# A two-layer encoder trunk: x turned raw, its modulation as columns, and the modulation products moved among the pointwise product's tiles

## The reference, cut to what matters

```python
c_act = silu(c)
mod = (c_act @ w_ada[l] + b_ada[l])              # 1024 x 6144 for each layer
sh1, sc1, g1, sh2, sc2, g2 = split(mod, 6)
h = x * (1 + sc1) + sh1
# layer 0: convolution block
u = h @ w_pw1 + b_pw1;  u = u[:, :D] * sigmoid(u[:, D:])     # "pointwise product"
y = depthwise_conv(u, w_dw, 31 taps, causal) + b_dw
y = silu(layer_norm(y)) @ w_pw2 + b_pw2
# layer 1: keys, values (with a modulation of their own, w_ada_kv), queries, attention, w_o
x = layer_norm(ALPHA * x + (1 + g1) * y)
h = x * (1 + sc2) + sh2
y = top2_of_16_experts(h)                        # three 1024 x 1024 matrices for each expert
x = layer_norm(ALPHA * x + (1 + g2) * y)
```

## Time and profile before

| what | value |
|---|---|
| median of 3 runs | 1354.38 us (1353.4 to 1354.49) |
| profiled execution, time | 1353.68 us |
| profiled execution, span of its rows | 1352.0 us |
| PE busy | 1132.6 us (84%) |
| DVE busy | 341.9 us (25%) |
| read from memory | 493.23 MB, 366 GB/s over the span |
| chain that ended last | PE 56%, DMA 37%, DVE 3% |

### The profile page before, as it was taken

The page is one execution under the profiler, slowest core; times in us unless marked ns, Lnnn a source line. Parts: engine busy times, 40 slices in busy tenths (PEclk is TensorE's granted clock), DMA queues, the critical chain, the costliest instruction groups (busy, mean ns, idle before and its releaser), DMA issues.

```text
span 1352.0 us, 16340 instructions
## 1 busy us (share of the span) xinstructions
PE 1132.6 (84%) x6426; PEld 486.6 (36%) x6426; DVE 341.9 (25%) x765; ACT 181.7 (13%) x325; POOL 23.1 (2%) x68
## 2 busy tenths in 40 slices
PE   2699998968998579677879999987899988886686
PEld 0486445322332123222265754532233322321222
DVE  0289433211212111111150152521211121111113
ACT  0001402101111000001010042210101011100001
POOL 3100100000000000000000000000000000000000
PEclk9699998988999889988989999789999999998798
DMA  9905989999999999999995344779999999999993
GB/s 372 409 8 210 419 342 429 424 426 428 427 425 425 427 427 426 426 427 426 421 418 208 125 187 156 304 309 426 427 427 426 395 419 423 429 427 424 429 426 159
DMA packets 43965, 495.70 MB, mean 367 GB/s; under 512 B 4554, under 2 KB 4570, under 8 KB 9570
## 3 DMA queue, kind: packets, MB, share of 16 engines
q1 hardware_dynamic: 42576, 490.75, 86.7%
q10 hardware_dynamic: 690, 2.34, 0.5%
q0 software_dynamic: 608, 1.21, 0.3%
HBM read 493.23 MB, written 1.05 MB: 366 GB/s over the span
## 4 chain that ended last, share of the span: by engine, by line
PE 56%; DMA 37%; DVE 3%; issue 2%; ACTq 1%; SPq 0%; POOL 0%; ACT 0%; POOLq 0%; DVEq 0%
DMA ring<-in_w_up_dram 23%; PE PS L1045 8%; DMA work<-in_w_up_dram 7%; PE PS L863 6%; PE PS L1001 6%; PE PS L1027 5%; PE PS L1142 4%; PE PS L881 4%; PE PS L1069 3%; PE PS L959 3%; PE PS L766 3%; DMA lnrows<-in_ln_ffn_b_dram 3%; DMA work<-in_w_down_dram 2%; PE PS L986 2%; DMA ring<-in_w_down_dram 2%
## 5 line engine op out<-in xcount | busy, mean ns | idle before, releaser
L1045 PE MATMUL PS<-ring,work 128*32 128x512 f32 x1184 | 169.2, 697 | 76.6 <-DMA ring<-in_w_up_dram 52.0
L1001 PE MATMUL PS<-ring,work 128*64 128x512 f32 x640 | 153.4, 624 | 28.6 <-DMA ring<-in_w_gate_dram 19.9
L1045 PEld LDWEIGHTS PS<-ring,work 128*32 128x32 f32 x1184 | 45.3, 125 | 194.8 <-issue 191.2
L1576 DVE TENSOR_TENSOR work<-work,PS 64x512 f32<-64x512 f32 x23 | 15.9, 692 | 320.4 <-ACT work L625 320.4
L1001 PEld LDWEIGHTS PS<-ring,work 128*64 128x64 f32 x640 | 47.0, 143 | 133.0 <-issue 117.1
L863 PE MATMUL PS<-ring,work 128*128 128x512 f32 x192 | 83.1, 593 | 0.0
L1045 PE MATMUL PS<-work 128*32 128x512 f32 x216 | 43.6, 702 | 38.3 <-DMA work<-in_w_up_dram 31.8
L986 PE MATMUL PS<-work 64*128 64x512 f32 x296 | 73.5, 615 | 1.6 <-DVE work L1553 1.6
L625 ACT ACTIVATE work<-PS 64x512 f32<-64x512 f32 x23 | 13.6, 590 | 435.9 <-PE PS L1045 435.9
L959 PE MATMUL PS<-hs,colv 128*64 128x512 f32 x296 | 72.0, 608 | 0.0
L766 PE MATMUL PS<-ring,crep 128*32 128x512 f32 x448 | 58.6, 670 | 15.1 <-DVE crep L1607 12.2
(11 more groups left out here) (276 smaller groups left out, 981.1 us busy)
## 6 DMA issues: line engine op xcount, KB each, us to landing
ring<-in_w_gate_dram SPq DMA_DIRECT2D x52, 2048.0 KB, 37.0
ring<-in_w_up_dram SPq DMA_DIRECT2D x52, 2048.0 KB, 40.5
ring<-in_w_down_dram SPq DMA_DIRECT2D x52, 2048.0 KB, 30.2
ring<-in_w_ada_dram SPq DMA_DIRECT2D x24, 2048.0 KB, 16.9
work<-in_w_gate_dram SPq DMA_DIRECT2D x12, 2048.0 KB, 27.2
ring<-in_w_pw_dram SPq DMA_DIRECT2D x6, 2048.0 KB, 39.6
xs<-in_w_up_dram SPq DMA_DIRECT2D x12, 1024.0 KB, 28.3
work<-in_w_up_dram SPq DMA_DIRECT2D x12, 1024.0 KB, 31.2
```

The lines of the kernel that those rows point to most:

```text
L1001: last = pe.matmul(PS[LARGE * half:LARGE * (half + 1), bank, :], XT[:, kk, LARGE * h:LARGE * (h + 1)], columns(tile, kk, half), start=(h = ...
L1045: last = pe.matmul(PS[SMALL * strip:SMALL * (strip + 1), GATE_BANK, :], XT[:, kk, LARGE * h:LARGE * h + SMALL], columns(load + 2 * h + str ...
```

## The change

1. **x is turned raw.** x is loaded into `hs` instead of `xs`. PE's first work is 16 transposes of it into banks 4 to 7, reading every fourth column. DVE copies x into `xs` in chunk order. After the first modulation third, the shift and scale go through `turn_mod` (4 products) into columns, and ACT and DVE write `hT = x^T * scale + shift` from the transposes. `spread_mod`, `modulate`, `turn_h` and `copy_hT` of this place are gone.
2. **The pointwise product goes tile by tile, with modulation products between.** The first three tiles take each chunk of `w_pw1` as it lands (order j, then f); the tap columns' work lies between these chunks. Then come the second modulation third's first load, tile 3, and the seven others of the second and last third in pairs behind tiles 3 to 6. The last third uses slots 0 to 3 again; so does the modulation of keys and values.
3. **The convolution's first tap** of tiles 0 to 4 moves from DVE to ACT (`begin_conv`); `DVE_STEPS` is a new table, with both `add_ada` in it.
4. **Keys' and values' modulation ahead of `w_pw2`**, in the order of loads and in PE's program: three of its loads lie before the last two products of the mean, one behind them. The mean takes six tiles before it. The bias of `w_pw2` is put first in its accumulation, beside the mean. `turn_ln` lies behind the variance.
5. The residual reads `xs` in contiguous rows; `add_ada` for keys and values is no longer inside the row norm.

```diff
-    L_PW2 = L_ADA0_G2 + ADA_G
-    L_ADAKV = L_PW2 + 2
-    L_ADA1_G0 = L_ADAKV + ADA_G
+    L_ADAKV = L_ADA0_G2 + ADA_G
+    L_PW2 = L_ADAKV + ADA_G
+    L_ADA1_G0 = L_PW2 + 2
...
+        if i in (L_ADA0_G2, L_ADA0_G2 + ADA_G):
+            waiting.rotate(ADA_G)
...
+    others = [i for i in range(LOADS) if layer_of(i) is None]
+    passed_on = others[:L_PW1] + others[L_ADA0_G1:L_ADA0_G2 + ADA_G] + others[L_PW1:L_ADA0_G1] + others[L_ADA0_G2 + ADA_G:]
...
-                act.dma_start(xs[:, t, :], x[0, t * P:(t + 1) * P, :]).then_inc(x_in, 16)
+                act.dma_start(hs[:, t, :], x[0, t * P:(t + 1) * P, :]).then_inc(x_in, 16)
...
-            copy_hT()
+            act.wait_ge(in_cols_copied, 1)
+            for b in (0, 2):
+                act.wait_ge(x_turned, b + 1)
+                for k in (2 * b, 2 * b + 1):
+                    last = act.activation(hT[:, k, :], PS[:, 4 + b, (k % 2) * SEQ:(k % 2 + 1) * SEQ], ACT.Identity,
+                                          scale=cols[:, SCALE, k:k + 1], bias=cols[:, SHIFT, k:k + 1])
+                last.then_inc(hT_even, 1)
+
+            def begin_conv(f):
+                act.wait_ge(u_ready, f + 1)
+                act.activation(CV[:, f, :], U[:, f, 0:SEQ], ACT.Identity, scale=colv[:, f, 0:1],
+                               bias=colv[:, f, ROW_BDW:ROW_BDW + 1]).then_inc(tap_begun, 1)
...
+            pe.wait_ge(x_in, 16 * TT)
+            for b in range(4):
+                for k in (2 * b, 2 * b + 1):
+                    h, kk = divmod(k, KH)
+                    for t in range(TT):
+                        last = pe.transpose(PS[:, 4 + b, (k % 2) * SEQ + t * P:(k % 2) * SEQ + (t + 1) * P],
+                                            hs[:, t, h * HALF + kk:(h + 1) * HALF:KH], ident[:, :])
+                last.then_inc(x_turned, 1)
             pe.wait_ge(c_spread, 1)
...
+            ada(L_ADA0_G0, 0)
             pe.wait_ge(ada_added, 1)
-            spread_mod(modv[0], 1, 4)
-            spread_mod(modv[0], 0, 6)
-            turn_ln(0, 2)
+            turn_mod(modv[0], (0,), TURNED_MODS, 1).then_inc(in_cols_turned, 1)
...
+            for j in range(4):
+                arrived(L_PW1 + j)
+                pe.wait_ge((hT_even, hT_odd)[j % 2], j // 2 + 1)
+                for f in range(3):
+                    gated(f, j)
+                if j == 0:
+                    turn_colrows()
+                if j == 1:
+                    spread_taps()
+            pe.wait_ge(u_ready, 2)
+            ada_load(L_ADA0_G1, 0, 1)
             pe.wait_ge(taps_copied, 3)
...
+            for f in range(3, KD):
+                for j in range(4):
+                    gated(f, j)
+                if f == 3:
+                    ada_load(L_ADA0_G1, 1, 1)
+                    ada_load(L_ADA0_G1, 2, 1)
+                if f == 4:
+                    ada_load(L_ADA0_G1, 3, 1)
+                    ada_load(L_ADA0_G2, 0, 0)
+                if f == 5:
+                    ada_load(L_ADA0_G2, 1, 0)
+                    ada_load(L_ADA0_G2, 2, 0)
+                if f == 6:
+                    ada_load(L_ADA0_G2, 3, 0)
...
-            ada(L_ADA0_G2, 6)
-            pe.wait_ge(ada_added, 2)
-            pe.wait_ge(later_in, LATER)
+            turn_ln(0, 7)
...
-            pe.wait_ge(ada_added, 3)
-            columns_and_turn(0, L_ADAKV)
+            project(L_PW2, 0, y_ready, z_ready, begun=True)
+            columns_and_turn(0, None)
...
-            add_residual(lambda t: [(by_chunk(xs[:, t, :])[:, h], chunks(t)[:, h]) for h in range(2)])
+            add_residual(lambda t: [(xs[:, t, :], hs[:, t, :])])
```

258 lines of the change are left out of this document (123 added, 135 removed).

## The result

The changed kernel takes 1344.16 us (median, 1339.37 to 1346.74), the kernel before in the same comparison 1353.4 us (1352.04 to 1354.49). The ratio is 0.9926, 95% interval 0.991 to 0.9942: faster by about 9 us. The forecast was 1333.5, range 1328 to 1341.5. So the direction was right, and the gain was less than half of what was forecast; the time lies outside the range. The profiled execution took 1346.74 us with a span of 1345.1 us, 6.9 us less than the span before (1352.0). Every median and ratio in this document is of the fast executions alone; one of the changed kernel (1872.01 us, in after_again) and one of the kernel before (2788.02 us) ran in a slower state and are left out.

A forecast was written before the change was run, and what follows sets the result against it. Layer 0's experts are bound by the weight stream, which waits for PE's arrival at the first expert. Arriving 19.3 us earlier plus 1.6 gives 20.9; 1353.7 - 20.9 = 1332.8, given as 1333.5, range 1328 to 1341.5.

The forecast's parts named there:

- X: How much earlier PE arrives at layer 0's first expert; forecast as 19.3 us.
- The term 1.6: At PE's first expert: the weight stream's 1.6 us of work left when slots come free, gained besides the earlier arrival.
- the others I estimate 5.1 us apart, 24.2 and 29.2: First modulation third: its third and fourth loads land at 24.2 and 29.2 us, so the product starts at 37.2.
- The bias, for which I kept a rival: Before `add_ada`: the bias's small load lands between 33 and 41, sliding PE's line by up to 8.2 us; chance 0.10.
- the 7.15 given: Pointwise product: its first chunk takes 7.15 us, including 1.97 charged once for a slow clock at the start.
- a clock at 0.50 past 45: Pointwise product: a granted clock of 0.50 past 45 us would show the forecast wrong.
- the rival of a penalty for each chunk: Product's first three tiles: the slow-clock penalty comes once a chunk, three more of 1.97 us, giving 1339.4; chance 0.05.
- 16.9 forecast: Convolution: PE needs 16.9 us for it, from the product's end at 110.8 to 127.8.
- 10.2 forecast, residual 2.36: Behind `w_pw2`: DVE's path falls from 12.8 to 10.2 us, with the residual at 2.36 and `add_ada` out.
- `w_pw2` at 27.7: PE's `w_pw2` product takes 27.7 us and ends at 176.0, 13.6 earlier than in the kernel before.
- nothing is changed: From DVE's columns to the first expert nothing changes, so the 19.3 us gained by then carries through.
- 2 better or 3 worse: Three modulation loads before the first expert, 7.05 us in the kernel before, may land 2 better or 3 worse.

The follow-up runs named there:

- after_again: The changed kernel run once more, unchanged: 1345.74 us, ratio 0.9937.
- kv_small_table: Changed kernel with `turn_ln` behind `w_pw2`, two key/value modulation loads one place later, ScalarE's and GpSimd's small loads later, an early one-column sigmoid: 1334.9 us.
- probe_before: The kernel before, with the third and fourth modulation loads taken ahead of the tap columns to show their landings; no time given.
- ln_kv: Changed kernel with `turn_ln` behind `w_pw2` and the last two key/value modulation loads one place later, one filling its old place: 1339.67 us.
- after_busy4: Changed kernel with four unused 512-column products on PE ahead of layer 0's transposes of h: 1339.45 us, ratio 0.9906.
- narrow8: Changed kernel with eight unused 4-column products on PE ahead of layer 0's transposes of h: 1341.79 us, ratio 0.9922.
- kept_busy_again: Second run of the changed kernel with an early one-column sigmoid and eight unused 512-column products ahead of layer 0's transposes of h: 1337.8 us.
- kept_busy: Changed kernel with an early one-column sigmoid and eight unused 512-column products ahead of layer 0's transposes of h: 1338.31 us, ratio 0.9894.

## Why the prediction was wrong in size and right in kind

**Right: what bounds the kernel.** "The whole gain is X + 1.6": X came out as 6.2 and the span fell by 6.9. The first expert product and the span move together over the variants that add no work (first 235.21, 229.01, 224.70, 221.81; span 1352.0, 1345.1, 1338.4, 1335.3); their difference lies between 1113.5 and 1116.8 in these and is 1118.0 in kv_small_table. The term 1.6 itself is too small to be told from these.

**Wrong: the landings, 5.4 us.** The step that failed first is "the others I estimate 5.1 us apart, 24.2 and 29.2". The loads were used at 27.70 and 34.64. The 5.1 us is a load's bytes over the stream's rate, which holds for eight loads together but not for the order in which they become whole. Of all landings only that of load 1 (18.79) ended a wait in the earlier trace rows; PE's first product waited for `crep`. probe_before shows that the kernel before has the same spacing, and that its rows hid it. Here the estimate was put on the critical path, where its error counted in full. Why the spacing is what it is stays open. The bias, for which I kept a rival, was on time: `add_ada` (0.75) stood directly behind the products of load 4.

**Wrong: the product's length, 3.4 us.** It took 77.0 (42.62 to 119.60) instead of 73.6. Chunk 0 took 1.2 more than the 7.15 given. That part is one execution's: in after_again it took 7.02, as forecast, and over the 18 profiles 7.02 to 8.40. The forecast's own sign of being wrong, a clock at 0.50 past 45, did come, partly because the product started late. The handover at tile 0 cost 1.1 (table load), which no step had. In the kernel before the load stands ahead of the wait for tile 0, which ends at 71.07, and costs nothing:

```profile
61.63 1.28 ACT L650 ACT_TABLE_LOAD   x1
```

In the changed kernel it stands behind that wait (65.18). The code ahead of the sigmoid has changed, it now waits for `cols_copied` as well; whether this moved the table load was not tested. The rest is 7.10 for a tile instead of 6.91.

**Right: the rival of a penalty for each chunk did not come.** Chunks 1 and 2 took 5.45 and 5.3 against the 5.18 of the full clock, and PE has no gap in front of them. The rule of the Trainium skill ("TensorE: Matmul & The Clock Gate", HAM oscillation) speaks of gaps in front of awaited slices; it bears on the loads ahead of the product, not on the chunks. There the trace agrees in part: the load at 19.20 took 1.92, the full clock, behind a wait of 3.43, and those at 27.70 and 34.64 took 3.64 and 3.50 behind waits of 6.58 and 3.30.

**Right: convolution and DVE.** PE's convolution took 17.1 (16.9 forecast), DVE's last tap ended 3.4 ahead of PE's last mean product (3 forecast), and from `w_pw2`'s end to h on DVE it took 10.3 (10.2 forecast, residual 2.36).

**Wrong: w_pw2 and what follows, 4.5 us.** I took `w_pw2` at 27.7 as in the earlier trace rows and said of the part up to the first expert "nothing is changed". No instruction there is changed, but what PE does ahead of them is: 4-column products now stand right before `w_pw2`, without a gap, and the gap before the transposes of h is 4 us wide. Granted clock 0.50 and 0.72 behind both: 1.7, 1.3 and 1.5 us. ln_kv shows the cause at `w_pw2`, after_busy4 and narrow8 at the transposes of h: 512-column products ahead bring the time back, narrow ones or a gap don't. The allowance "2 better or 3 worse" for the routing was there, but the one for `w_pw2` was missing, and all bounds of the range leaned on landings that were already wrong.

**The range.** It ended at 1341.5, made of one late term at a time. Four terms came together, all late: the landings 5.4, the product 3.4, `w_pw2` 1.7, and what follows it 2.8.

## What to carry to other kernels

If a change puts the landing of early loads on the critical path, a rate times bytes is no landing time: move a consumer ahead in the kernel before and read the waits. Count the clock for every PE stage behind narrow products or a gap of some us, even if the stage itself isn't touched; wide work in its place gives most of it back. And when two kernels differ where none of their instructions do, look at how much code lies ahead: sixteen instructions (and their weight loads) were worth some 9 us of layer 1 in the profiles, more than several of the edits.

## What the hardware showed that was not expected

- **Early loads.** The second, third and fourth load of 2 MB, issued together, land 8.1 to 8.7 and 5.9 to 6.9 us apart in either kernel (19 profiles), where a load's bytes over 426 GB/s are 4.9; neither 16 small loads of one queue nor four loads instead of eight in flight matter; GpSimd's small loads cost some 2 us.
- **Code.** On entering layer 1's experts PE stands still for 3.8 us in the midst of a product (5.4 to 6.2 in the 14 profiles with the wait for DVE), and the clock falls to half (6.39 for a product of 3.64); with 16 more instructions ahead it is 1.5 and 3.64. The page of the changed kernel counts the queue as

```profile
q8 instruction: 81, 1.33, 0.4%
```

  81 packets of some 16 KB: too little traffic to notice.
- **Clock.** 4-column products don't hold it: it was 0.50 from 190 to 212 in narrow8. In layer 1's routing it was at 0.50 for some 20 us in the changed kernel and kept_busy_again and for 6 in kept_busy, the same kernel, which was worth 3.6 us; what decides that stayed open, and with it why executions of one kernel spread by 3 to 13 us.
- **Table load.** It took 1.28 us each time. It can stand ahead of the wait of the activation that needs it (61.63 in the kernel before) or behind it (65.18 in the changed kernel), where it is on the critical path; a sigmoid of one column in an idle time took it off. The Trainium skill gives 1283 ns for it ("ScalarE: Activation LUTs", What ACT_TABLE_LOAD costs); the trace agrees.
